# Ten modulation sums and nine weight roundings change place in a two-block transformer kernel

## The reference

```python
mod = jax.nn.silu(c) @ w_ada[l] + b_ada[l]            # 6 x 1024 modulation values per block
sh1, sc1, g1, sh2, sc2, g2 = jnp.split(mod[:, None, :], N_MOD, axis=-1)
u = rmsnorm(h, norm1_w[l]) * (1.0 + sc1) + sh1
proj = u @ w_in[l]
...
o_hg = hgrn2(hq, hf, hi, hg, lower_bounds[l], hgrn_gnorm_w[l])
o_da = diff_attention(aq, ak, av, lam, lambda_init, diff_subln_w[l])
mix = jnp.concatenate([o_hg, o_da.astype(o_hg.dtype)], axis=-1) @ w_out[l]
h = h + g1 * mix
u = rmsnorm(h, norm2_w[l]) * (1.0 + sc2) + sh2
ff = (jax.nn.silu(u @ w_ffn_gate[l]) * (u @ w_ffn_up[l])) @ w_ffn_down[l]
```

## Time and profile before

| | |
|---|---|
| median of 3 runs | 1551.96 us (1550.62 to 1553.38) |
| the profiled execution | 1551.1 us, span of the trace 1549.4 us |
| PE busy | 1471.8 us, 95% of the span |
| DVE busy | 986.4 us, 64% |
| ACT busy | 443.6 us, 29% |
| attention steps | 212.8 to 309.95 us from the span's start |
| `out1a` 3 to 7 and `out1` 0 | 309.95 to 328.67 us |

### The profile page before, as it was taken

How to read it: one execution, slowest core, us unless ns; L and a number is a source line. 1 busy time by engine, 2 the same in 40 slices (tenths; PEclk the granted TensorE clock), 3 DMA queues, 4 the chain that set the end, 5 groups by cost and what they waited for, 6 DMA issues and landing times.

```text
span 1549.4 us, 19554 instructions
## 1 busy us (share of the span) xinstructions
PE 1471.8 (95%) x7190; PEld 1174.2 (76%) x7190; DVE 986.4 (64%) x1720; ACT 443.6 (29%) x913; POOL 95.5 (6%) x75
## 2 busy tenths in 40 slices
PE   4989998898999999998999999999998999999997
PEld 2877876576888888887876666778886888888886
DVE  6888878777766766567546666876555444444342
ACT  4234344433222221002234545531113222222011
POOL 0100000020000000221700000000030000000110
PEclk7999999999999999999999999999999999999999
DMA  9243224333656565444221111113332223233332
GB/s 359 82 164 102 75 86 133 109 96 127 197 191 198 182 202 171 144 137 133 69 81 43 42 42 42 55 49 102 105 99 68 95 95 104 86 108 88 98 90 92
DMA packets 52610, 175.80 MB, mean 113 GB/s; under 512 B 5952, under 2 KB 6336, under 8 KB 52544
## 3 DMA queue, kind: packets, MB, share of 16 engines
q1 hardware_dynamic: 52544, 174.94, 34.9%
HBM read 172.82 MB, written 2.10 MB: 113 GB/s over the span
## 4 chain that ended last, share of the span: by engine, by line
PE 51%; ACT 1%; DVE 1%; issue 0%; ACTq 0%; DVEq 0%
PE bank L619 11%; PE bank L621 11%; PE bank L620 11%; PE bank L1059 8%; PE bank L1078 2%; PE bank L1113 2%; PE bank L1090 2%; PE bank L631 1%; PE bank L633 1%; PE bank L632 1%; PE bank L990 0%; DVE wl L1589 0%; PE bank L1103 0%; PE bank L1034 0%; PE bank L695 0%
## 5 line engine op out<-in xcount | busy, mean ns | idle before, releaser
L619 PE MATMUL bank<-uh,wh 128*128 128x512 f32 x808 | 316.2, 391 | 5.9 <-DVE wl L1589 4.8
L621 PE MATMUL bank<-uh,wl 128*128 128x512 f32 x808 | 315.4, 390 | 0.0
L620 PE MATMUL bank<-ul,wh 128*128 128x512 f32 x808 | 315.2, 390 | 0.0
L1587 DVE CAST wh<-wraw 128x1024 fp32r<-128x1024 f32 (+1 forms) x235 | 156.0, 664 | 198.4 <-PE bank L621 179.9
L1589 DVE TENSOR_TENSOR wl<-wraw,wh 128x1024 fp32r<-128x1024 f32 (+1 forms) x235 | 274.0, 1166 | 8.1
L619 PEld LDWEIGHTS bank<-uh,wh 128*128 128x128 f32 x808 | 152.1, 188 | 39.0 <-issue 4.9
L620 PEld LDWEIGHTS bank<-ul,wh 128*128 128x128 f32 x808 | 152.2, 188 | 31.5
L621 PEld LDWEIGHTS bank<-uh,wl 128*128 128x128 f32 x808 | 152.0, 188 | 31.4
L619 PE MATMUL bank<-hh,wh 128*128 128x512 f32 x352 | 137.6, 391 | 0.0
L621 PE MATMUL bank<-hh,wl 128*128 128x512 f32 x352 | 137.1, 390 | 0.0
L620 PE MATMUL bank<-hl,wh 128*128 128x512 f32 x352 | 137.1, 389 | 0.0
(11 more groups left out here) (350 smaller groups left out, 2379.0 us busy)
## 6 DMA issues: line engine op xcount, KB each, us to landing
ada<-in_w_ada_dram SPq DMA_DIRECT2D x96, 512.0 KB, 4.6
wraw<-in_w_in_dram SPq DMA_DIRECT2D x61, 512.0 KB, 3.3
wraw<-in_w_ffn_gate_dram SPq DMA_DIRECT2D x44, 512.0 KB, 3.3
wraw<-in_w_ffn_up_dram SPq DMA_DIRECT2D x44, 512.0 KB, 3.3
wraw<-in_w_ffn_down_dram SPq DMA_DIRECT2D x32, 512.0 KB, 3.5
wraw<-in_w_ffn_down_dram SPq DMA_DIRECT2D x16, 384.0 KB, 3.1
wraw<-in_w_out_dram SPq DMA_DIRECT2D x16, 256.0 KB, 2.7
wraw<-in_w_out_dram SPq DMA_DIRECT2D x8, 512.0 KB, 3.3
```

Of the source, the lines that this page charges most:

```text
L619: nc.tensor.matmul(bank[:], a, rh[:, k0 + k, :], start=(first and k == 0), stop=False)
L620: nc.tensor.matmul(bank[:], a, rl[:, k0 + k, :], start=False, stop=False)
L621: mm = nc.tensor.matmul(bank[:], b, rh[:, k0 + k, :], start=False, stop=(last and k == nk - 1))
L1587: V.tensor_copy(wh[:, slot, 0:n], wraw[:, slot, 0:n]).then_inc(w_hi, 1)
```

## The change

The table `MOD_AFTER` is rewritten. Each of the five `da1` splits is followed by one sum where there were two (pieces 24 to 28), the splits of `out1a` 0, 1 and 2 by none where there were two, and that of `out1a` 3 by piece 29. The ten pieces 30 to 39 come two at a time behind the splits of `out1a` 4 to 7 and of `out1` 0. The transfers of the pieces move with them.

For the nine units in `CAST_A` (`da1` 1 to 5 and `out1a` 0 to 3; `da1` 0 is not among them) VectorE no longer rounds. ScalarE does it, in the new function `cast`, at the end of its even steps 0 to 16, with the same waits and one more (`w_split`, for the split before). VectorE still waits for `w_hi` and subtracts.

```diff
--- before.py
+++ after.py
@@ -337,9 +337,12 @@
 
         MOD_AFTER = {PH["a1"].u0 + n + 1: [15 + n] for n in range(1, 9)}
         for n_ in range(5):
-            MOD_AFTER[PH["da1"].u0 + n_ + 1] = [24 + 2 * n_, 25 + 2 * n_]
-        for n_ in range(3):
-            MOD_AFTER[PH["out1a"].u0 + n_] = [34 + 2 * n_, 35 + 2 * n_]
+            MOD_AFTER[PH["da1"].u0 + n_ + 1] = [24 + n_]
+        MOD_AFTER[PH["out1a"].u0 + 3] = [29]
+        for n_ in range(4, 8):
+            MOD_AFTER[PH["out1a"].u0 + n_] = [22 + 2 * n_, 23 + 2 * n_]
+        MOD_AFTER[PH["out1"].u0] = [38, 39]
+        CAST_A = {PH["da1"].u0 + n_ for n_ in range(1, 6)} | {PH["out1a"].u0 + n_ for n_ in range(4)}
         for n_ in range(22):
             MOD_AFTER[PH["ff1"].u0 + 2 * n_ + 2] = [40 + 2 * n_, 41 + 2 * n_]
         for n_ in range(12):
@@ -1373,6 +1376,14 @@
                     A(junk1[:, 0:P], clamped[:, c * P:(c + 1) * P], ACT.Square, scale=SQ_SCALE,
                       accum_out=ssh[:, 16 + 4 * h + c:17 + 4 * h + c]).then_inc(ss_ok, 1)
 
+            def cast(u, nk):
+
+                n, slot = nk * P, u % 2
+                act.wait_ge(w_in[slot], 16 * (u // 2 + 1 - FRONT // 2))
+                act.wait_ge(unit_done, u - 1 + U1)
+                act.wait_ge(w_split, u)
+                A(wh[:, slot, 0:n], wraw[:, slot, 0:n], ACT.Copy).then_inc(w_hi, 1)
+
             for m in range(DA_TILES_N + 3):
                 if m - 1 in HG_AT:
                     h = HG_AT[m - 1]
@@ -1396,6 +1407,11 @@
                     n = m // 2
                     act.wait_ge(unit_done, PH["da1"].u0 + n + 1 + U1)
                     A(p1[:, TILES["da1"][n], :], B[1][:], ACT.Copy).then_inc(drain_a, 1)
+                if m < DA_TILES_N + 2 and m % 2 == 0:
+                    if m < 10:
+                        cast(PH["da1"].u0 + m // 2 + 1, KT)
+                    elif m < 18:
+                        cast(PH["out1a"].u0 + (m - 10) // 2, NT)
             nc.scalar.preload_act_table(ACT.Sqrt)
             output_squares(HEADS1 - 1)
             act.wait_ge(rs_ok, 5)
@@ -1584,7 +1600,8 @@
                 else:
                     v.wait_ge(unit_done, u - 1 + U1)
                 n = nk * P
-                V.tensor_copy(wh[:, slot, 0:n], wraw[:, slot, 0:n]).then_inc(w_hi, 1)
+                if not isinstance(u, int) or u not in CAST_A:
+                    V.tensor_copy(wh[:, slot, 0:n], wraw[:, slot, 0:n]).then_inc(w_hi, 1)
                 v.wait_ge(w_hi, u + 1)
                 V.tensor_tensor(wl[:, slot, 0:n], wraw[:, slot, 0:n], wh[:, slot, 0:n].bitcast(F32),
                                 ALU.subtract).then_inc(w_split, 1)
```

## The result

The kernel after takes 1553.82 us (median of 20 runs, 1551.29 to 1557.12), the kernel before, timed beside it, 1551.64 us (20 runs, 1550.28 to 1553.63). The ratio is 1.0014 with a 95% interval of 1.0009 to 1.0020: no change by the bound of 0.2%, and slower by some 2 us on a closer look. The profiled execution of the kernel after took 1552.81 us with a span of 1551.0; that of before 1551.1 and 1549.4.

The account below looks back on a forecast made before the run. It took PE, busy 95% of the span, as the bound, with VectorE setting the pace in the first half of the steps. Steps -9.2 and projection +9.6 gave +0.4 on 1551.1, taken as 1552.0 us, range 1549.5 to 1554.5 (8 in 10: 1548.0 to 1555.5).

Parts of the forecast that it names:

- two large terms: Attention steps end 9.2 us earlier; the projection behind them loses 9.6 us to ten sums on VectorE's chain.
- Step 0: First attention step: VectorE stands until ScalarE rounds, so PE's wait at 224.35 grows from 3.05 to 5.5 us.
- Steps 2 to 8: Attention steps: each pair takes VectorE 1.9 us less, 9.8 and 9.6; PE's 2.88 us wait at 257.88 should go.
- Steps 10 to 16: Late attention steps: each pair loses 2.8 us on VectorE; PE's 4.07 us wait at 301.48 should go.
- Waits and clock: Attention steps: PE waits fall from 15.4 to 10.9 us, and the clock's cost from 7.2 to 2.5.
- The small waits: PE's waits in the attention steps other than the three large ones: all 5.4 us kept.
- Rival A: Faster: the steps' small waits fall to about 1 us, the steps gain 13.6, total 1547.1 to 1548; chance 0.18.
- The price of the first fall: Attention steps: the one clock fall left, behind the longer first PE wait, costs 2.5 us.
- The chain: Projection: VectorE's work from the clamp to the end of `out1` 1's split grows from 17.17 to 27.6 us.
- The transfers: Loads of the moved pieces, passed later in SyncE's queue: costed at nothing; a late piece would add up to 2 us.
- Rival C: Slower: the clock falls in the projection at `out1` 0 and 1, +4.6 us at most, 1554.5 to 1556; chance 0.12.
- Rival B: Slower: ScalarE rounds too late behind a copy needing PE's transposition, steps gain 4 to 5 us, total 1556; chance 0.12.

Follow-up runs that it names:

- sums only: The changed kernel with all roundings back on VectorE, so only the ten sums move: 1548.40 us, ratio 0.9979 to the kernel before.
- Two moved: Against sums only, piece 38 goes behind the split of `out1` 1, piece 39 and the gains behind the next normalization's statistics: 1547.81 us.
- tail casts: Against Two moved, ScalarE does the five roundings of `out1a` 4 to 7 and `out1` 0 in the projection: 1546.61 us.
- Narrow tail: The changed kernel with the ten projection sums reading 128 of 1024 columns, transfers whole, second normalization's scale wrong: 1547.08 us.
- the kernel with all edits: Against tail casts, ScalarE also does eight roundings (`da1` 2 to 5, `out1a` 0 to 3) right behind its exponentials: 1545.02 us.

## Why the prediction was right

The forecast was no change at 1552.0, and the kernel came out at 1553.8, 2.2 above its neighbour, inside the narrower range of 1549.5 to 1554.5. Its two large terms held: -9.2 in the steps came out as -8.7 and +9.6 in the projection as +9.7, and the experiments show that the sums cause both. Inside the first term some parts were off in opposite directions, and that they cancelled was luck; it is said with each.

- **Step 0.** Predicted a wait of 5.5 us, measured 5.70. VectorE goes on to the scores of step 1 at 224.19 (224.2 predicted).
- **Steps 2 to 8.** The wait at 257.88 fell from 2.88 to 1.08 (under 2 predicted). The pace was only half right: the first pair of steps takes VectorE 9.8 us as predicted (232.91 to 242.68), the second 10.85 instead of 9.6 (to 253.53), with 0.63 us of it a wait for ScalarE's rounding.
- **Steps 10 to 16.** The wait of 4.07 was to go and became 2.10, just over the bound of 2, and the clock fell once more behind it (0.77 over 7.46 us, 1.7 us). Piece 29 was covered as costed: VectorE still waits 1.50 us for PE behind it.
- **Waits and clock.** 11.1 us of waits beside 10.9; the clock cost 77.37 - 74.5 = 2.9 us beside 2.5. The clamp came at 301.89 beside 301.4. Both totals owe something to luck. The small waits, kept at 5.4 us, are 11.1 - 5.7 = 5.4; but 3.2 of these are what was left of the two large ones (1.08 and 2.10), and the small ones themselves fell to 2.1 (1.02 and 1.09). And the 2.5 us of clock were one fall behind the first wait: that one cost 1.4 (0.65 over 4.08 us), and the second fall, which was not forecast, the rest. Rival A, that the 5.4 us go to about 1, is out as a total, but about the small waits it was nearer; and the gain of 13.6 that it gave the steps is what sums only reached (14.3).
- **The price of the first fall** is itself not shown. Two moved and tail casts have the same program in the steps. Behind the first wait the clock was 1.00 in the one (223.62 to 228.20) and 0.63 in the other (223.92 to 228.50), and the clamp comes 79.0 and 79.1 us from the common start: there the fall cost nothing.
- **The chain.** 27.6 us predicted, 27.6 measured. PE's waits in it for the subtraction add up to only 6.0 us, not 9: in 301.25 to 329.50 it is idle for 28.25 - 21.64 = 6.6 us, and busy for 3.1 us more than the 18.56 of the earlier trace rows, 1.7 of which is the clock behind 325.11 (0.37 x 4.64); the other 1.4 are not explained. Narrow tail shows that the ten sums are the cause.
- **The transfers.** Nothing, as costed. In the kernel after, the view of waits has no wait for a transfer between 212 and 335 us.
- **Rival C** came true in part. Behind the wait of 2.99 us the clock was 0.63 over `out1` 0, 1.7 us; but VectorE's split of `out1` 1 ended only 0.26 us before PE did, so the rest was hidden, and 0.1 more came with the next unit. By the Trainium skill ("TensorE: Matmul & The Clock Gate", section "A second HAM failure mode: psum-queue depth-cycling") the short waits should do this too; the stretch 301.25 to 319.99, with waits of up to 1.74 us, is at 1.00.

From the sum of +0.4 to the 2.2 measured: the steps gained 8.7 at the clamp instead of 9.2, which makes +0.9 at the first addition, and +1.0 at the second with the clock's rest. The profiled spans differ by 1.6 us and the medians by 2.2. What is added behind 333 us was not looked for.

What the prediction had wrong is inside a term that came out right. It counted the nine roundings as 5.1 us of relief and only the first as a loss. By the experiments they are a loss of 5.4 us: 3.2 from the first, 2.2 from the other eight (4.0 and 1.8 at the clamp). The gain in the steps belongs to the sums alone, and they would have given 14.3 (the clamp at 296.26). Rival B, held at 0.12, named this mechanism, with roundings behind a copy that needs PE's transposition; it priced the later roundings at about 4.5 us, and they cost 2.2. But it was put as a question of whether the steps still gain enough, and they did, because the sums gain more. Its mechanism is shown in part: VectorE's waits for ScalarE halve when the roundings move ahead of the copy (7.8 to 3.6 us), but the clamp gains only 0.5 of the 1.8 us by it. The argument against it, that ScalarE waits for VectorE anyway in later steps, is what failed: VectorE stood 7.7 us in seven places for the later roundings. A reason that fits, but that no run isolates, is that ScalarE's rounding stands behind the exponentials that follow VectorE's maxima.

## What to carry to other kernels

Price the two halves of a change separately, each against the kernel with the other already in: a total near zero can hide a part that costs 5 us. Giving work to an engine that is 29% busy helps only if that engine reaches it before the owner would have; read its queue at that moment, not its share of the span. And take work off an engine where it is the bound (the projection, here) rather than where it waits already.

## What the runs showed of the hardware

VectorE and GpSimd hold each other's instructions. With GpSimd adding 128 x 512 float32 values in 1.39 to 1.59 us, the VectorE instruction that began inside it took 2.31 us instead of 1.28 (the sum), 1.51 instead of 0.42 (the rounding) or 1.66 instead of 0.69 (the subtraction): 1.0 to 1.1 us each. The addition to `res`, which reads PSUM, was not held (0.75). The other direction shows in the kernel before, where VectorE's subtraction began first and GpSimd took 2.24 us instead of 1.47:

```profile
346.58 1.23 DVE L1589 TENSOR_TENSOR wl<-wraw,wh 128x1024 fp32r<-128x1024 f32 x1
```

```profile
346.68 2.24 POOL L533 TENSOR_TENSOR ssq<-ssq,sq 128x512 f32<-128x512 f32 x1 [1.25 <-ACT sq L1197]
```

In a unit of 2.72 us with 0.9 to spare this is the difference between hidden and not.

One wait does not decide the clock. Behind 2.96 us it was 0.50 through the unit in sums only, behind 2.99 us 0.63 in the kernel after, behind 2.51 us 0.63 in tail casts, and behind 2.52 us, at the same place in nearly the same program, 1.00 in the kernel with all edits. The last large wait of the steps tells the same: behind 2.10 us 0.77 in the kernel after, behind 2.09 us 1.00 in narrow tail (294.48 to 300.36), behind 1.80 us 0.72 in the kernel with all edits (289.95 to 296.00). An estimate for such a place needs both values, here 0 and 2.5 us apart.
